# Expert stages of a two-layer encoder: shorter place sums, constant products before them, weights in halves

## The reference

```python
g_val, g_idx = lax.top_k(softmax(t @ w_group + b_group), 1)          # 1 of 4 groups
e_val, e_idx = lax.top_k(softmax(chosen), 2)                          # 2 of its 8 experts
for g in range(N_GROUPS):                                             # all 32 experts, 1024 x 256
    a = einsum('td,edf->tef', t, w_gate[g]); u = einsum('td,edf->tef', t, w_up[g])
    y = y + einsum('tef,efd->td', silu(a) * u * combine[:, g, :, None], w_down[g])
```

## Time and profile before

| | |
|---|---|
| median of 3 runs | 876.13 us (876.10 to 878.23) |
| the profiled execution: its time, its span | 876.75 us, 875.0 us |
| PE busy | 776.4 us (89%) |
| VectorE, ScalarE, GpSimd busy | 395.4, 237.9, 191.0 us |
| read from memory | 243.16 MB, 280 GB/s over the span |
| gate/up products, L1794 | 231.0 us busy, 604 ns mean |
| down products, L1825 | 116.9 us busy, 598 ns mean |

### The profile page before, as it was taken

The page is one execution under the profiler, slowest core; times in us unless marked ns, Lnnn a source line. Parts: engine busy times, 40 slices in busy tenths (PEclk is TensorE's granted clock), DMA queues, the critical chain, the costliest instruction groups (busy, mean ns, idle before and its releaser), DMA issues.

```text
span 875.0 us, 10464 instructions
## 1 busy us (share of the span) xinstructions
PE 776.4 (89%) x3995; PEld 425.9 (49%) x3995; DVE 395.4 (45%) x720; ACT 237.9 (27%) x422; POOL 191.0 (22%) x198
## 2 busy tenths in 40 slices
PE   2667879599999998999999878996999999998997
PEld 1556734543433333346878654545533343333456
DVE  6996742623232322136668658515322232222264
ACT  3323123331111101016575444422310111100153
POOL 5874500221110110000056364002211011010000
PEclk9988979699999999999999959996999999999999
DMA  6035070979999999996787660175199999999761
GB/s 217 1 56 194 5 289 1 390 281 425 421 421 420 421 421 419 422 411 218 260 209 248 250 194 1 54 300 223 57 422 421 420 421 422 421 420 421 321 253 48
DMA packets 61091, 245.46 MB, mean 281 GB/s; under 512 B 19667, under 2 KB 20721, under 8 KB 36081
## 3 DMA queue, kind: packets, MB, share of 16 engines
q1 hardware_dynamic: 56752, 240.36, 69.1%
q0 software_dynamic: 1600, 4.26, 2.1%
q10 hardware_dynamic: 2688, 0.17, 0.2%
HBM read 243.16 MB, written 1.60 MB: 280 GB/s over the span
## 4 chain that ended last, share of the span: by engine, by line
PE 83%; DVE 7%; issue 5%; ACT 2%; POOL 2%; DMA 1%; SPq 0%; ACTq 0%; DVEq 0%; POOLq 0%
PE PS L1794 26%; PE PS L1825 13%; PE PS L1545 10%; PE PS L1835 7%; PE PS L1727 3%; PE PS L2008 3%; PE PS L1765 2%; PE PS L1669 2%; PE PS L1967 2%; PE PS L1988 2%; PE PS L1603 2%; PE PS L1915 2%; PE PS L1806 1%; PE PS L1684 1%; POOL qrs L685 1%
## 5 line engine op out<-in xcount | busy, mean ns | idle before, releaser
L1794 PE MATMUL PS<-ring,xe 128*64 128x512 f32 x1024 | 231.0, 604 | 15.9 <-issue 13.5
L1794 PEld LDWEIGHTS PS<-ring,xe 128*64 128x64 f32 x1024 | 79.8, 139 | 163.7 <-issue 163.7
L1825 PE MATMUL PS<-ring,actT 128*64 128x512 f32 x512 | 116.9, 598 | 1.7 <-DVE actT L1303 1.4
L612 POOL COPY xe<-xg 128x512 f32 x60 | 47.1, 786 | 300.1 <-PE PS L1794 297.7
L1317 DVE TENSOR_TENSOR olo<-PS,ohi 128x512 fp32r<-128x512 f32 x64 | 44.3, 692 | 123.5 <-ACT ohi L855 123.5
L1303 DVE COPY actT<-PS 128x256 f32<-128x256 f32 x32 | 13.6, 425 | 175.6 <-PE PS L1806 175.6
L855 ACT ACTIVATE ohi<-PS 128x512 fp32r<-128x512 f32 x64 | 38.3, 598 | 153.0 <-PE PS L1825 153.0
L1008 DVE SCALAR_TENSOR_TENSOR ringr<-ring,gT,dwh 128x512 fp32r<-128x512 f32 x80 | 62.9, 838 | 26.7 <-ACT dwh L726 25.4
L847 ACT ACTIVATE act<-PS 128x256 f32<-128x256 f32 x32 | 12.3, 385 | 225.5 <-PE PS L1794 225.5
L1825 PEld LDWEIGHTS PS<-ring,actT 128*64 128x64 f32 x512 | 34.7, 136 | 67.1 <-issue 67.1
L1545 PE MATMUL PS<-ringr,rawh 128*128 128x512 f32 x160 | 63.4, 396 | 0.8 <-DVE ringr L1008 0.8
(11 more groups left out here) (323 smaller groups left out, 1031.3 us busy)
## 6 DMA issues: line engine op xcount, KB each, us to landing
ring<-in_moe_w_gate SPq DMA_DIRECT2D x64, 1024.0 KB
ring<-in_moe_w_up SPq DMA_DIRECT2D x64, 1024.0 KB
ring<-in_moe_w_down SPq DMA_DIRECT2D x64, 1024.0 KB, 24.2
ring<-in_nat_w_qkv SPq DMA_DIRECT2D x6, 2048.0 KB
ring<-in_ple_w_gate SPq DMA_DIRECT2D x4, 2048.0 KB
ring<-in_s_w_out SPq DMA_DIRECT2D x2, 2048.0 KB
ring<-in_nat_w_o SPq DMA_DIRECT2D x2, 2048.0 KB
ring<-in_s_w_in SPq DMA_DIRECT2D x1, 2048.0 KB
```

The costliest lines, as they stand in the source:

```text
L612: pool.tensor_copy(xe[:, e % 4, :, :], xg[:, :, bass.ds(first, CAP)]).then_inc(S("xe_ready"), 1)
L1794: ins = mm(PS[CAP * h_:CAP * h_ + CAP, 0, :].rearrange("p (u f) -> p u f", u=2), xe[:, (2 * p + h_) % 4, k, :], wv[h_][:, k], start=k == 0 ...
L1825: ins = mm(PS[CAP * h_:CAP * h_ + CAP, 2 + n, :], actT[:, k, CAP * h_:CAP * h_ + CAP], wd[h_][:, k, 512 * n:512 * n + 512], start=k == 0, ...
```

## The change

Four things, made together. The masks become one fp32r tensor `mb`, with `tri` and `ones` in fp32r too; the place sums go from seven float32 products to four in fp32r, the tally from four to two. `constant(n)` issues n fp32r products of ones by ones, 512 columns, into bank 6 of PSUM, whose result nothing reads: 2 before the second router product, 24 between it and the place sums, 5 behind them. `spread_rows` moves from before pair 0's gate/up to between its halves. Gate and up weights are loaded in two halves of 4 KB for each partition (slices 0 to 3 and 4 to 7), and PE waits for the second half only at slice 4; the first halves of pair p are issued at the new `gu_half` of pair p - 3, the second ones at its `gu_done`. Several semaphores are merged (s5_T, angle_steps, u_moved, table_moved), to have names for the new ones; `ones` is read as float32 again where the products stay float32.

```diff
-        tri = new("tri", [P, P])
+        tri = new("tri", [P, P], F32R)
-        ones = new("ones", [P, P])
+        ones = new("ones", [P, P], F32R)
...
+        def later_arrived(eng, n):
+            eng.wait_ge(later[items[n][0]], 32 * nth_moe[n])
...
-        msk = at("msk", [P, TT, NE], F32, RX + 2432)
-        below = at("below", [P, TT, NE], F32, RX + 2688)
+        mb = at("mb", [P, TT, 2, NE], F32R, RX + 2432)
+        msk, below = mb[:, :, 0], mb[:, :, 1]
...
-                sp.dma_start(ring[s][:, 0:2048], gate_[1]).then_inc(loaded[s], 32)
-                sp.dma_start(ring[s][:, 2048:4096], up_[1]).then_inc(loaded[s], 16)
+                for half, sem in enumerate((loaded[s], later[s])):
+                    cs = slice(1024 * half, 1024 * half + 1024)
+                    sp.dma_start(ring[s][:, 0:2048][:, cs], gate_[1][:, cs]).then_inc(sem, 16 if half else 32)
+                    sp.dma_start(ring[s][:, 2048:4096][:, cs], up_[1][:, cs]).then_inc(sem, 16)
+
+            def load_pair(n):
+
+                i, e = (0, n - moe_item[0]) if n < moe_item[1] else (1, n - moe_item[1])
+                for half in range(2):
+                    sp.wait_ge(S("gu_done" if half else "gu_half"), NP * i + e // 2 - 2)
+                    for m in (n, n + 1):
+                        s, (gate_, up_, down_) = items[m]
+                        cs = slice(1024 * half, 1024 * half + 1024)
+                        sem = later[s] if half else loaded[s]
+                        sp.dma_start(ring[s][:, 0:2048][:, cs], gate_[1][:, cs]).then_inc(sem, 16 if half else 32)
+                        sp.dma_start(ring[s][:, 2048:4096][:, cs], up_[1][:, cs]).then_inc(sem, 16)
...
-                        load_gate_up(m0 + 2 * p, False)
-                        load_gate_up(m0 + 2 * p + 1, False)
+                        load_pair(m0 + 2 * p)
...
                 pe.wait_ge(S("msk_ready"), i + 1)
+                dst = PS[:, 4, 0:TT * NE].rearrange("p (t e) -> p t e", t=TT)
                 for t in range(TT):
-                    dst = PS[:, 4, NE * t:NE * t + NE]
-                    mm(dst, ones[:, :], below[:, 0], start=True, stop=False)
-                    mm(dst, ones[:, :], below[:, 1], start=False, stop=False)
-                    if t:
-                        mm(dst, ones[:, :], msk[:, 0], start=False, stop=False)
-                    ins = mm(dst, tri[:, :], msk[:, t], start=False, stop=True)
-                ins.then_inc(S("pos_done"), 1)
-                for w, of in enumerate((msk, below)):
-                    for t in range(TT):
-                        ins = mm(PS[:, 5, 64 + NE * w:64 + NE * w + NE], ones[:, :], of[:, t], start=t == 0, stop=t == 1)
+                    mm(dst, ones[:, :], bc(mb[:, t, 1], 1, TT), start=t == 0, stop=False)
+                mm(dst[:, 1], ones[:, :], mb[:, 0, 0], start=False, stop=False)
+                mm(dst, tri[:, :], msk, start=False, stop=True).then_inc(S("pos_done"), 1)
+                for t in range(TT):
+                    ins = mm(PS[:, 5, 64:64 + 2 * NE], ones[:, :], mb[:, t].rearrange("p w e -> p (w e)"),
+                             start=t == 0, stop=t == 1)
                 ins.then_inc(S("tally_done"), 1)
+
+            def constant(n):
+
+                for _ in range(n):
+                    mm(PS[:, 6, :].rearrange("p (b n) -> p b n", b=4), ones[:, :], bc(ones[:, :], 1, 4),
+                       start=True, stop=True)
...
                     if k0 == 0:
                         arrived(pe, it)
+                    else:
+                        later_arrived(pe, it)
...
-                if k1 == KD:
-                    ins.then_inc(S("gu_done"), 1)
+                ins.then_inc(S("gu_done" if k1 == KD else "gu_half"), 1)
...
                 x_T(i, 1)
+                constant(2)
                 router(i, 1)
+                constant(24)
                 places(i)
+                constant(5)
...
-                spread_rows(i)
                 for p in range(NP):
                     gate_up(i, p, 0, 4)
+                    if p == 0:
+                        spread_rows(i)
                     gate_up(i, p, 4, KD)
```

More of the change, by code:

```diff
@@ L216, in program @@
         down_loaded = [S(f"down_loaded{s}") for s in range(6)]
+        later = [S(f"later_loaded{s}") for s in range(6)]
         nth_moe, cnt_ = {}, {}
@@ L426, in load, with load_gate_up @@
                     sp.dma_start(dst, src).then_inc(loaded[s], 48 - 16 * (len(parts) - 1) if j == 0 else 16)
-            def load_gate_up(n, first):
+            def load_gate_up(n):
                 s, (gate_, up_, down_) = items[n]
[L431 to L434, removed]
+                if prev[n] is not None:
                     name, value = done[prev[n]]
                     sp.wait_ge(S(name), value)
-                sp.dma_start(ring[s][:, 0:2048], gate_[1]).then_inc(loaded[s], 32)
-                sp.dma_start(ring[s][:, 2048:4096], up_[1]).then_inc(loaded[s], 16)
+                for half, sem in enumerate((loaded[s], later[s])):
[12 more added lines that the diff above has]
+                        sp.dma_start(ring[s][:, 2048:4096][:, cs], up_[1][:, cs]).then_inc(sem, 16)
             def load_down(n, first):
@@ L534, in _ @@
             pool.memset(mask[:, :], 1.0)
-            pool.memset(tri[:, :], 1.0)
-            pool.memset(ones[:, :], 1.0)
+            pool.memset(tri[:, :].bitcast(F32), 1.0)
+            pool.memset(ones[:, :].bitcast(F32), 1.0)
             link(pool.memset(negh[:, :], 0.0))
@@ L1225, in route @@
                         ALU.is_gt))
-                tt(msk[:, :, :], eq[:, :, 0], eq[:, :, 1], ALU.add)
-                tt(below[:, :, :], low[:, :, 0], low[:, :, 1], ALU.add).then_inc(S("msk_ready"), 1)
+                tt(msk, eq[:, :, 0], eq[:, :, 1], ALU.add)
+                tt(below, low[:, :, 0], low[:, :, 1], ALU.add).then_inc(S("msk_ready"), 1)
                 ts(ngm[:, :], gmx[:, :, 0], -1.0, None, ALU.mult)
@@ L1644, in _ @@
                 weights_T(n)
-            pe.wait_ge(S("us_loaded"), 16 * L)
+            pe.wait_ge(S("u_moved"), 16 + 16 * L)
             inputs(0)
@@ L1676, in _ @@
             for k in range(2):
-                mm(PS[:, 6 + k, :].rearrange("p (b n) -> p b n", b=4), zrow[:, :], bc(ones[0:1, :], 1, 4),
+                mm(PS[:, 6 + k, :].rearrange("p (b n) -> p b n", b=4), zrow[:, :], bc(ones[0:1, :].bitcast(F32), 1, 4),
                    start=True, stop=False)
@@ L1773, in spread_rows @@
                     pe.wait_ge(S("diag_ready"), 2 * TT * i + TT * n + TT)
-                    mm(PS[:, 2 + n, :], ones[:, :], diag[:, n].rearrange("p j t s -> p (j t s)"), start=True, stop=True)\
+                    mm(PS[:, 2 + n, :], ones[:, :].bitcast(F32), diag[:, n].rearrange("p j t s -> p (j t s)"), start=True, stop=True)\
                         .then_inc(S("row_done"), 1)
```

52 lines of the change are left out of this document (26 added, 26 removed).

## The result

The changed kernel takes 867.15 us (median of 4 runs, 866.13 to 868.72), the kernel before 876.12 beside it: ratio 0.989, 95% interval 0.987 to 0.992. That is faster, by 9.0 us; 21 were forecast, with a range that ended at 864. The profiled execution of the changed kernel is 868.72 us, its span 867.0 against 875.0.

The account below looks back on a forecast made before the run. The weight stream, about 421 GB/s, was taken as the bound, its restart behind the preload deciding a stage's end. Stage 1 -9.3 and stage 2 -12.0 sum to -21.3, 0.3 given back: 855 us from 876.13, range 850 to 864.

Parts of the forecast that it names:

- the row products in the shadow: Row products behind pair 0's first half: copies and weights they wait for fit, by 2 us or more.
- half arrival: PE starts a product on its first halves; pair 15 ends 3.5 us after its last byte, gaining 3.5 us a stage.
- Rival 3: Halves don't overlap in PE's gate/up products, only the earlier start counts: -14, 862 us; chance 0.08.
- rival 4: The weight stream pays for each transfer, four more a pair; at 0.3 us each slower, 886 us; chance 0.04.
- Rival 4's sign: The per-transfer price was to be decided by the expert stages' plateau falling below about 380 GB/s.
- Step "half transfers": Gate/up loads: rows shrink from 8 KB to 4 KB, costing between none and 3% of 129.5 us a stage.
- the term of 1%: Loss taken for 4 KB rows in the gate/up loads: 1.3 us a stage, bounds 0 and 3.9.
- Rival 1: Half transfers flow slower than same-shape rows did: at 395 GB/s 869 us, at 3% loss 860; chance 0.16.
- priced as a hole: Stage 2's stream start: second halves issued 5.4 us behind first halves that flow 5.0 us, a gap of 0.5 us.
- Step "constant products": Between router and gathers they keep PE's clock up; gathers cost 7.3 us, gaining 1.8 in stage 1, 2.5 in stage 2.
- Stage 2: -12.0: Second expert stage's forecast change in us: -9.8 earlier start, +1.3 half transfers, -3.5 half arrival.
- Stage 1: -9.3: First expert stage's forecast change in us: -7.1 hole closed, +1.3 half transfers, -3.5 half arrival.

Follow-up runs that it names:

- e1_rows_4k: The kernel before, gate and up still in 1 MB transfers but writing rows of 4 KB; 884.7 us, ratio 1.008.
- e14_rows_of_512: The changed kernel with the width reordered over partitions and slices, so each half matrix is one 0.5 MB stretch of memory; 865.3 us, ratio 0.987.
- e3_whole: The changed kernel with whole gate and up transfers again, asked for at gu_done; 867.8 us, ratio 0.990 to the kernel before.
- e6_const12: The changed kernel with 12 constant products behind the place sums in place of 5; 865.05 us, ratio 0.987 to the kernel before.
- e15_big_strided: The changed kernel with 1 MB transfers at gu_done, from pair 3 on reading every second 4 KB of two matrices; output not the layer's; 888.5 us.
- e10_preload_whole: The changed kernel with the six preloaded experts in whole transfers, halves from pair 3 on; 865.95 us, ratio 0.986 to the kernel before.

## Why the prediction was wrong

**Right.** The bound (the stream behind the preload), the order of events, and every PE step but one: place sums 0.7 us against 0.8; the constants at 0.24 us each inside the idle time; the row products in the shadow, halves 5.5 us apart; no empty microsecond in stage 1 from 155 to 375; half arrival, where pair 15 ends 3.65 us behind its last bytes, 3.4 us a stage. ScalarE waits 1.14 us at 395.82 for PLE's weights where it had 0.34, and 3.36 us in stage 2, and what follows each stage moves with it. Rival 3 is out, and rival 4 with it: no price per transfer shows, since the plateau is 413 at ten transfers a pair as at six (e1_rows_4k). Rival 4's sign, a plateau below about 380, didn't follow from its own prices: 0.2 and 0.3 us for each transfer make 400 and 390 GB/s of a pair's 6.29 MB. The Trainium skill, DMA: Bandwidth & Descriptors, in its cost section, would have 0.524 MB over 2.0 + 1.2 us, 164 GB/s, if its fixed part were paid in the stream (an estimate from its figures); the trace does not agree, here as in the kernel before.

**Step "half transfers", the term of 1%.** Rival 1 came, in a mild form and with an addition that no part of the prediction had. Gate/up bytes took their loss by rows: plateau 413 for 421. Between the start and pair 15's last bytes lie 80 MB in stage 1 and 72 MB in stage 2, and by 80/0.413 - 80/0.421 = 3.7 us and 3.3 us they cost 2.4 and 2.0 more than the 1.3 put in. I had bounded it rightly, by 3% of the gate/up bytes, and took the value nearest to a row of one microsecond, which can't tell 2%: single microseconds of the changed kernel's plateau read 385 to 463. The trace of the kernel before had more to say of that very shape. The first w_out load, from its second microsecond of flow on:

```profile
67.00:72.00 5.00, 4.57 (x39) 3.56 (x40) 0.84 (x1) 4.23 (x8) 5.00 (x2) 1.00 0.98 394
```

The row that I took is one of the two best microseconds of the second such load; 394 over these five was the warning, also for the start of a stream.

**The same step, the start.** I let the stream start at the plateau's rate. In stage 2 it moved 6.18 MB in 20 us against 7.80: at 421 GB/s 3.8 us, of which 0.5 was priced as a hole and 0.9 is the rows'. In stage 1 the preload lost 0.54 MB in 16 us, and 0.64 by 28 us, 1.5 us. For stage 2's start the runs put 0.38 MB of the 1.62 on the rows (e1_rows_4k) and 0.6 to 1.0 on the pattern of addresses (e14_rows_of_512 against its match). In the preload the rows account for 0.32 MB of the 0.54, the pattern for about 0.1, and the rest is open.

**Step "constant products".** They hold the clock from the router to the place sums, as forecast. The step failed at "the five behind the sums hide in the 3.1 us": they fill 1.2 of them and leave 1.8, in which the clock falls. The gathers gained 0.2 and 0.7 us where 1.8 and 2.5 were counted, and stage 2's stream starts 8.4 us nearer to its preload's first issue (44.2 before, 35.8 now), not 10.3.

**The sums again.** Stage 2: -12.0 + 1.9 (start) + 3.3 (slow start beyond the hole) + 2.0 (plateau) = -4.8, measured -4.3. The rows' part of the slow start, 0.9, is in the 3.3 and not in the 2.0, which counts from 20 us on. Stage 1: -9.3 + 1.5 + 2.4 = -5.4, measured -3.3; 2 us of it I can't place. From the preload's first issue to the landing of pair 15's last bytes 91.0 MB flow in the kernel before, 90.9 in e1_rows_4k and 91.1 in e3_whole, but 91.7 in the changed kernel and 91.2 in e6_const12. So it seems that bytes which belong behind pair 15 came first, at 421 GB/s up to 1.7 us of them; why was not tried. Outside the stages 0.6 us of upstream shift came free. The forecast's range held the milder half of rival 1, and ended 3 us short.

## What to carry to other kernels

Splitting transfers to start them earlier also changes their rows and the addresses in flight together: price both, over every byte of the stream, and split only the transfers whose early start or late end is waited for. Where halves are needed, let each be one stretch of memory: here that gave 1.9 us. Work that is to hold the clock should reach up to the next real product: here the clock fell in the 1.8 us that the constants left open, and not when 0.2 us were left. And price a stream by its mean over many microseconds, its start included, not by its best one.

## What the runs showed of the hardware

- Rows of 4 KB in place of 8 KB cost 2% of a full stream: 413 against 421 GB/s, with six transfers a pair and with ten alike.
- Reading every second 4 KB of memory, in the first 20 us from an empty queue: in transfers of 1 MB 6.60 MB against 7.42 (e15_big_strided, e1_rows_4k), in transfers of 0.5 MB 6.2 to 6.6 against 7.22 (changed kernel, e10_preload_whole; e14_rows_of_512). In the plateau nothing of it is left: 413 with both.
- Gate and up in transfers over 64 partitions in place of 128, with 8 KB rows, the down weights over 128 as before: 239 GB/s against 421 (e2_twice).
- The clock fell from 2.4 to 1.2 GHz in a wait of 1.8 us behind the place sums and five constants, in both stages, and not in one of 0.2 us behind the place sums and twelve (e6_const12).
